# A ring of ten half places for the expert weights of a decoder layer, with the pair's products in another order

## The reference, cut to what matters

```python
h = h + merged @ w_out                       # end of the mixer
xt = rmsnorm(h, g_ffn)
logits = xt @ w_router + b_router            # top 4 of 32, softmax over the four
...
for each block of one expert e:              # rows = its tokens
    g = minimum(xb @ w_gate[e] + b_gate[e], 7.0)
    u = clip(xb @ w_up[e] + b_up[e], -7.0, 7.0)
    act = g * sigmoid(1.702 * g) * (u + 1.0)
    y[rows] += (act @ w_down[e] + b_down[e]) * wts
```

## Time and profile before

| | us |
|---|---|
| runs shown | 1229.80, 1230.49, 1230.92; median 1230.49 |
| profiled execution | 1230.71 |
| its span from the first to the last instruction | 1228.9 |
| PE busy | 1160.3 (94% of the span) |
| DMA, mean busy share of the 16 engines from about 305 to 1205 us | 0.98 to 1.03 |

### The profile page before, as it was taken

How to read it: one execution, slowest core, us unless ns; L and a number is a source line. 1 busy time by engine, 2 the same in 40 slices (tenths; PEclk the granted TensorE clock), 3 DMA queues, 4 the chain that set the end, 5 groups by cost and what they waited for, 6 DMA issues and landing times.

```text
span 1228.9 us, 13742 instructions
## 1 busy us (share of the span) xinstructions
PE 1160.3 (94%) x5460; PEld 586.8 (48%) x5460; DVE 446.5 (36%) x775; ACT 249.7 (20%) x409; POOL 47.6 (4%) x72
## 2 busy tenths in 40 slices
PE   8999999999999999999999899989999989899998
PEld 5888888787343443434343333424343424343433
DVE  4878798765312131231312131212222121212122
ACT  5555577632110100010010001000110000010000
POOL 2222100200000000000000000000000000000000
PEclk9999999999999999999999999999999999999999
DMA  9454545487999999999999999999999999999994
GB/s 374 146 197 171 189 154 206 169 341 305 429 422 428 428 431 429 437 428 429 438 430 428 434 434 428 430 437 430 428 433 434 429 429 434 434 425 436 434 423 189
DMA packets 28143, 458.59 MB, mean 373 GB/s; under 512 B 3216, under 2 KB 4112, under 8 KB 6608
## 3 DMA queue, kind: packets, MB, share of 16 engines
q1 hardware_dynamic: 26720, 454.14, 87.7%
q0 software_dynamic: 1104, 3.93, 1.0%
q10 hardware_dynamic: 288, 0.10, 0.0%
HBM read 457.11 MB, written 1.05 MB: 373 GB/s over the span
## 4 chain that ended last, share of the span: by engine, by line
PE 66%; DMA 27%; DVE 4%; ACT 1%; issue 1%; POOL 0%; SPq 0%; DVEq 0%; POOLq 0%
PE bank L1712 26%; DMA experts_ring<-in_w_up 25%; PE bank L1423 16%; PE bank L1754 11%; PE bank L1700 4%; PE bank L1640 3%; DMA back<-in_mixer_halves 2%; PE bank L1718 2%; PE bank L1387 1%; DVE back_split L913 1%; PE bank L1719 1%; DVE region L1337 1%; ACT region L891 0%; ACT region L896 0%; ACT back_split L653 0%
## 5 line engine op out<-in xcount | busy, mean ns | idle before, releaser
L1712 PE MATMUL bank<-experts_ring,region 128*64 128x512 f32 x2048 | 455.1, 597 | 28.2 <-DMA experts_ring<-in_w_up 14.4
L1712 PEld LDWEIGHTS bank<-experts_ring,region 128*64 128x64 f32 x2048 | 148.3, 137 | 312.1 <-issue 290.2
L1754 PE MATMUL bank<-experts_ring,region 128*64 128x512 f32 x1024 | 226.8, 595 | 14.3 <-ACT region L891 14.3
L1423 PE MATMUL bank<-back_split,region_split 128*128 128x512 f32 x600 | 176.6, 396 | 0.2
L1754 PEld LDWEIGHTS bank<-experts_ring,region 128*64 128x64 f32 x1024 | 75.6, 137 | 143.1 <-issue 129.1
L1423 PEld LDWEIGHTS bank<-back_split,region_split 128*128 128x128 f32 x600 | 110.5, 188 | 25.1 <-issue 2.0
L1372 DVE COPY region<-bank 64x512 f32<-64x512 f32 x32 | 22.2, 694 | 227.3 <-PE bank L1754 227.3
L913 DVE TENSOR_TENSOR back_split<-back,back_split 128x2048 fp32r<-128x2048 f32 x34 | 77.9, 2291 | 32.4 <-ACT back_split L653 32.2
L1423 PE MATMUL bank<-back_split,front_split 128*128 128x512 f32 x216 | 84.4, 391 | 0.0
L1361 DVE TENSOR_SCALAR region<-bank 128x512 f32<-128x512 f32 x32 | 22.1, 691 | 163.4 <-PE bank L1719 163.4
L884 ACT ACTIVATE region<-region 128x512 f32<-128x512 f32 x32 | 20.1, 630 | 292.0 <-DVE region L1354 292.0
(11 more groups left out here) (174 smaller groups left out, 790.1 us busy)
## 6 DMA issues: line engine op xcount, KB each, us to landing
experts_ring<-in_w_gate SPq DMA_DIRECT2D x26, 4096.0 KB, 32.5
experts_ring<-in_w_up SPq DMA_DIRECT2D x22, 4096.0 KB, 33.9
experts_ring<-in_w_down SPq DMA_DIRECT2D x20, 4096.0 KB, 35.1
experts_ring<-in_w_down SPq DMA_DIRECT2D x24, 2048.0 KB, 21.4
experts_ring<-in_w_up SPq DMA_DIRECT2D x20, 2048.0 KB, 16.0
back<-in_mixer_halves SPq DMA_DIRECT2D x36, 1024.0 KB, 4.8
experts_ring<-in_w_gate SPq DMA_DIRECT2D x12, 2048.0 KB, 12.3
front<-in_mixer_halves SPq DMA_DIRECT2D x8, 1024.0 KB, 4.8
```

Source lines behind the costliest of these rows:

```text
L1423: ins = nc.tensor.matmul(UB[u % 3][:, :], a[:, k, toks], b[:, cols], start=(k == 0 and m == 0), stop=(k == k_n - 1 and m == 2))
L1712: ins = nc.tensor.matmul(dst[h * SLOTS:(h + 1) * SLOTS, :], XE[:, kk, e * SLOTS:(e + 1) * SLOTS], w[:, k, h * HALF:(h + 1) * HALF], start= ...
L1754: ins = nc.tensor.matmul(bank[2][h * SLOTS:(h + 1) * SLOTS, :], AHT[:, k, half * SLOTS:(half + 1) * SLOTS], w[:, k, h * HALF:(h + 1) * HAL ...
```

## The change

The ring has ten half places instead of nine, so no piece wraps, and a load waits for half `g-10`. The mixer's buffers lie in SBUF in another order, and the small expert tiles have moved into regions that the ring does not cover. The first two pairs (`BY_HALVES`) and the whole last pair go by halves, the very last half as two quarters; pieces between are whole. The first halves are released otherwise: g=1 behind the load of H=39, g=2 behind that of H=40, g=3 after `wba1`, g=4 to 8 one after the other as halves of `wo0` and `wo1` are used, g=9 after the logits. The biases are loaded right behind g=0.

On PE, the dispatch of the next pair follows the first gate product; the wait for the upper half of the tokens stands between the halves of that product; combining is cut in two, one part behind the first up product and one inside the second gate product; the first turned activations come before the second up product, the second ones inside the first down product, through bank 0 and a second copy `AHT[1]`; the second down product has bank 1. The final combining uses four banks. GpSimd's clearing of `PWT` waits for the routing.

```diff
-RING = 9
+RING = 10
-TURN_PAIRS = 3
+TURN_PAIRS = 5
+BY_HALVES = 2 * PER_PAIR
+LAST_PAIR = PER_ROUND - PER_PAIR
...
+        buffers = ("region9", "mem_low", "x_low", "region7", "hi4", "raw4", "region8", "hi0", "raw0", "hi1",
+                   "raw1", "hi2", "raw2", "hi3", "raw3", "region1", "region10", "region2",
+                   "region0", "region5", "region3", "region4", "region6")
...
             def stream(pair, n, was_used):
-                if place(2 * n) == RING - 1:
-                    for g in (2 * n, 2 * n + 1):
-                        sp.wait_ge(used, was_used + (g + 1 - RING))
-                        load_half(pair, g)
-                else:
-                    sp.wait_ge(used, was_used + (2 * n + 2 - RING))
-                    load_piece(pair, n)
+                sp.wait_ge(used, was_used + (2 * n + 2 - RING))
+                load_piece(pair, n)
...
-                for n in range(TURNS * PER_TURN // 2, PER_ROUND // 2 - 1):
-                    stream(PAIRS - 1, n, was_used)
-                for g in (PER_ROUND - 2, PER_ROUND - 1):
+                for g in range(LAST_PAIR, PER_ROUND - 1):
                     sp.wait_ge(used, was_used + (g + 1 - RING))
                     load_half(PAIRS - 1, g)
+                sp.wait_ge(used, was_used + (PER_ROUND - RING))
+                rest = expert_rows(PAIRS - 1, PER_ROUND // 2 - 1)[:, 4096:8192]
+                for i in range(2):
+                    part = slice(i * 2048, (i + 1) * 2048)
+                    sp.dma_start(ring_half(PER_ROUND - 1)[:, part], rest[:, part]).then_inc(last_in[PER_PAIR - 1 + i], 16)
             for H in range(HALVES, 2 * N0):
                 load(H)
                 if H == 2 * PIECES.index("wba1"):
                     sp.wait_ge(pv_done, HEADS)
                     sp.wait_ge(merged, 4)
                     load_half(0, 0)
+                    biases()
+                if H == 2 * PIECES.index("wba1") + 1:
+                    sp.wait_ge(oT_done, HEADS)
+                    load_half(0, 1)
                 if H == 2 * PIECES.index("wo0"):
                     sp.wait_ge(unit_done, UNIT_OF[("ga1", NT - 1, 0)] + 1)
-                    biases()
-                    load_half(0, 1)
-            for g, name in enumerate(("wba1", "merged", "wo0", "wo0", "wo1", "wo1", "logits"), 2):
...
+                    load_half(0, 2)
+            sp.wait_ge(unit_done, UNIT_OF[("wba1", NT - 1, 0)] + 1)
+            load_half(0, 3)
+            sp.wait_ge(mgT_done, 4)
+            half_free(sp, 2 * PIECES.index("wo0"))
+            load_half(0, 4)
+            half_free(sp, 2 * PIECES.index("wo0") + 1)
+            load_half(0, 5)
+            half_free(sp, 2 * PIECES.index("wo1"))
+            load_half(0, 6)
+            half_free(sp, 2 * PIECES.index("wo1") + 1)
+            load_half(0, 7)
+            load_half(0, 8)
+            sp.wait_ge(logit_done, NT)
+            load_half(0, 9)
...
             def pair_products(r, d, s):
                 it = r * PAIRS + d * TURN_PAIRS + s
                 pe.wait_ge(xe_lo, it + 1)
-                pe.wait_ge(xe_hi, it + 1)
-                project(it, r, d, s, 0, 0, 0, bank[0])
+                project(it, r, d, s, 0, 0, 0, bank[0], lambda: pe.wait_ge(xe_hi, it + 1))
+                dispatch(it + 1)
...
+                pe.wait_ge(o_lo, it * 2 + 2)
+                pe.wait_ge(o_hi, it * 2 + 2)
                 project(it, r, d, s, 0, 1, 2, bank[1])
-                combine(it)
+                combine(it, 0)
                 pe.wait_ge(g_read, it * 2 + 1)
-                project(it, r, d, s, 1, 0, 4, bank[0])
+                project(it, r, d, s, 1, 0, 4, bank[0], lambda: combine(it, 1))
                 pe.wait_ge(u_read, it * 2 + 1)
+                pe.wait_ge(act_ready, it * 2 + 1)
+                pe.wait_ge(wT_copied, it + 2)
+                turn4(bank[3], [AH[:, j * P:(j + 1) * P] for j in range(4)], actT_done)
                 project(it, r, d, s, 1, 1, 6, bank[1])
                 for e in range(2):
-                    pe.wait_ge(act_ready, it * 2 + (e + 1))
-                    if e == 0:
-                        pe.wait_ge(wT_copied, it + 2)
-                    turn4(bank[3], [AH[:, e, j * P:(j + 1) * P] for j in range(4)], actT_done)
-                    if e == 0:
-                        dispatch(it + 1)
-                    if e == 1:
-                        pe.wait_ge(o_lo, it * 2 + 3)
-                        pe.wait_ge(o_hi, it * 2 + 3)
                     pe.wait_ge(actT_copied, it * 2 + (e + 1))
...
+                        if j == 8:
+                            pe.wait_ge(act_ready, it * 2 + 2)
+                            turn4(bank[0], [AH[:, b * P:(b + 1) * P] for b in range(4)], actT_done)
...
-            combine(n_rounds * PAIRS)
+            for j in range(4):
+                t, h = divmod(j, 2)
+                if j < 2:
+                    pe.wait_ge(y_added, last * 4 + (j + 1))
+                nc.tensor.matmul(bank[(6, 7, 0, 2)[j]][:, :], PWT[:, t * P:(t + 1) * P], OE[:, h * HALF:(h + 1) * HALF],
+                                 start=True, stop=True).then_inc(comb_done, 1)
```

More of the change, by code:

```diff
@@ L191, in decoder_layer @@
             named("attention_buffers", [P, 4096])
[L192 to L195, removed]
+            plain = {name: named(name, [P, 2048]) for name in buffers}
+            extra = named("extra", [P, HALF])
+            con = named("con", [P, C_ALL])
         prob = sb("prob", [P, 2, 768])
@@ L199, in decoder_layer @@
         rot = sb("rot", [P, 2, 2, NT, HD])
[L200 to L211, removed]
+        split_of = {name: sb(name + "_split", [P, 2048], F32R) for name in buffers}
+        extra_r = sb("extra_split", [P, HALF], F32R)
+        sb("con_kept", [P, C_MASK])
+        con_r = sb("con_split", [P, HALF], F32R)
+        region = [plain[f"region{i}"] for i in range(11)]
+        region_r = [split_of[f"region{i}"] for i in range(11)]
         small = sb("small", [P, 68])
@@ L330, in decoder_layer @@
         second_in = [sem(f"second_in{i}") for i in range(RING)]
-        last_in = [sem(f"last_in{i}") for i in range(2)]
+        last_in = [sem(f"last_in{i}") for i in range(PER_PAIR + 1)]
         gbias_in = [sem(f"gbias_in{i}") for i in range(3)]
@@ L396, in place @@
             return g % RING
-        whole_starts = [place(2 * n) for n in range(PER_ROUND // 2 - 1)]
+        whole_starts = [place(2 * n) for n in range(LAST_PAIR // 2)]
         def in_round(s):
@@ L413, in wait_half @@
             n, h = divmod(g, 2)
-            if n == PER_ROUND // 2 - 1:
-                pe.wait_ge(last_in[h], r * 16 + 16)
+            if g >= LAST_PAIR:
+                pe.wait_ge(last_in[g - LAST_PAIR], r * 16 + 16)
             elif h == 0:
                 pe.wait_ge(piece_in[place(g)], landed(r, d, n))
-            elif place(g) == 0:
-                pe.wait_ge(second_in[RING - 1], landed(r, d, n))
-            elif n < PER_TURN // 2:
+            elif g < BY_HALVES:
                 pe.wait_ge(second_in[place(g - 1)], 16 * whole_starts[:n + 1].count(place(g - 1)))
@@ L458, in load_half @@
                 n, h = divmod(g, 2)
-                if n == PER_ROUND // 2 - 1:
-                    landing = last_in[h]
+                if g >= LAST_PAIR:
+                    landing = last_in[g - LAST_PAIR]
                 else:
@@ L524, in _ @@
                         load_piece(0, n)
-                    load_half(0, RING - 1)
-                    sp.wait_ge(used, r * PER_ROUND + 1)
-                    load_half(0, RING)
-                    for n in range(RING // 2 + 1, PER_TURN // 2):
+                    for n in range(RING // 2, PER_TURN // 2):
                         stream(n // (PER_PAIR // 2), n, r * PER_ROUND)
@@ L859, in logit_exp, with xe_lower_half @@
                 nc.scalar.activation(GATE[:, t, :], LG[:, t, :], ACT.Exp, bias=stat[:, 180 + t:181 + t]).then_inc(lexp_done, 1)
-            def xe_lower_half(n):
+            def xe_lower_half(n, after):
                 act.wait_ge(disp_done, n * 2 + 1)
+                if after is not None:
+                    act.wait_ge(used, after)
                 nc.scalar.activation(XE[:, 0:4, :], bank[4][:, :].rearrange("p (k n) -> p k n", k=4),
@@ L890, in _ @@
                             act.wait_ge(actT_done, it * 2 + (e + 1))
-                            nc.scalar.activation(AHT, bank[3][:, :].rearrange("p (j s) -> p j s", j=4),
+                            nc.scalar.activation(AHT[e], bank[(3, 0)[e]][:, :].rearrange("p (j s) -> p j s", j=4),
                                                  ACT.Copy).then_inc(actT_copied, 1)
                             if e == 0:
-                                xe_lower_half(it + 1)
+                                xe_lower_half(it + 1, it * PER_PAIR + 8)
+                        for e in range(2):
                             act.wait_ge(used, it * PER_PAIR + (10 + 2 * e))
```

(14 more changed lines are left out.)

99 lines of the change are left out of this document (48 added, 51 removed).

## The result

The changed kernel takes 1233.15 us (median of 14 runs, 1231.63 to 1235.05), the kernel before 1230.22 (14 runs, 1228.48 to 1232.49). The ratio is 1.0022, 95% interval [1.0015, 1.0029]: slower by 0.22%, about 2.7 us by the ratio (the medians differ by 2.9). The forecast was 1226.2 in a range of 1220 to 1229.5, so the time lies above the range. The profiled execution took 1235.05 us with a span of 1233.3.

What follows compares the result with a forecast made beforehand. Weight DMA was taken to bound the experts, PE the end. Last landing 1212.5 + 4.9 - 4.9 + 2 = 1214.5; plus 2.4 + 7.7 gives span 1224.6, plus 1.8 - 0.2 gives 1226.2 us; range 1220 to 1229.5.

Steps and rivals of the forecast that it cites:

- the layout ... nothing: Whole kernel: the buffers' new layout, with GpSimd's later clearing, moved biases and split token wait, changes the time by nothing.
- Earlier expert halves: Mixer's end: g=2 ahead of H=41 delays S, the first expert product, by 4.9 us, 311.55 to 316.4; bounds 0 and 4.9.
- The step on H=40: Mixer's end: H=40 lands about 6 us later, but its split is done before H=41 arrives.
- The queue's order: SP's load queue at the mixer's end: loads land in order of issue, and no landing overtakes another.
- rival (a): Mixer's end: H=41 is not held up, S stays at 311.55, E is 4.9 us earlier, time 1221.3; chance 0.17.
- The dispatch moves forward: First pairs: 3.57 us of dispatch delay giving back ring places, so E, the last weight landing, is 2 us later; bounds 0, 3.3.
- The prediction's own test: Sign that the middle was wrong: DMA share under 0.95 anywhere from 330 to 450 us.
- The tenth place: Start of the expert stream: nine other halves issued instead of eight, so E comes 4.9 us earlier; bounds 0 and 4.9.
- Whole pieces from the third pair: Third pair on: a whole piece waits for two places at once; cost taken as 0, bounds 0 and 3.5 us.
- Less waiting within a pair: Expert pairs: 16 x 0.9 us of waits for ACT's copy and gaps in combining go, worth nothing until the last pair.
- rival (c): Expert pairs: PE becomes the bound, a pair taking over 58.4 us instead of the 54 expected; 1242 us; chance 0.08.
- The last pair and the banks: Kernel's end: last product at E + 2.4, final combining in four banks 7.7 us to the end, instead of 8.1.

Runs made afterwards that it cites:

- e3: The kernel before with only PE's loop over turns written out, so its instructions stream in: 1235.5 us, ratio 1.0048 to the kernel before.
- e5: Changed kernel with g=1, g=2 and biases released as before the change and the dispatch back behind the second up product: 1224.48 us, 0.9953 of the kernel before.
- e7: Changed kernel with nine half places, three-pair turns, the old release of early loads and dispatch behind the second up product: 1225.52 us, 0.9963 of the kernel before.
- e8: Changed kernel with only the bias loads put back behind H=40, g=1 and g=2 still early: 1232.61 us, 1.0016 of the kernel before.
- e9: Changed kernel with only the dispatch moved back behind the second up product, early releases kept: 1230.9 us, 1.0002 of the kernel before.
- e2: Changed kernel with g=1, g=2 and the biases released as before the change: 1228.78 us, 0.9984 of the kernel before.
- e1: Changed kernel with only g=2 moved back behind wba1, just ahead of g=3: 1231.36 us, 1.0003 of the kernel before.
- e6: Changed kernel with nine half places, three-pair turns and the old release of early loads, dispatch still early: 1227.73 us, 0.9977 of the kernel before.
- e4: The kernel before with only its last pair by halves and the last half in two quarters: 1227.0 us, 0.9971 of the kernel before.

## Why the prediction was wrong, by its steps

**The five-pair loop** is the step that cost the forecast most. It was not a term at all: the diff's `TURN_PAIRS = 5` was read as bookkeeping of the ring, and "the layout ... nothing" was where it belonged. From the 36th landing to the last the kernel before takes 758.3 us, the changed kernel 764.3: 6.0 us, where the forecast had none. e3 shows 5.2 of it without any other change, e5 against e7 5.4.

**Earlier expert halves** (S + 4.9): direction right, size wrong in the profile, where S came 8.2 later. The step that failed is the price, "One more half of 2 MB ahead of it costs 4.9 us": H=41 took 6.8 us longer (14.90 instead of 8.09) and was issued 0.4 later. At most about 1 us of the difference is the biases' place (e8); the rest stays open. Behind that, one tile of the dispatch took 3.16 us instead of 2.03, at the lower granted clock again (0.57 from 311 to 315 us): 1.1 of the 8.2. Why the clock fell there, with PE busy for 5.0 of the 6 us ahead of it, no run tells. Other executions come nearer to the forecast: counted from the issue of H=38, S is 7.9 us later after and 5.1 in e9, with the same front, and the medians put the front at 4.7 us (after to e2) and 6.0 (e9 to e5).

The step on H=40, "its split is done before H=41's arrives", held in the changed kernel: H=40's lower part was ready at 270.6, 3.1 us before H=41 landed.

```profile
268.26 2.29 DVE L914 TENSOR_TENSOR raw_split<-raw,hi_split 128x2048 fp32r<-128x2048 f32 x1 [5.36 <-ACT hi_split L651]
```

But that hid a second loss. H=40 landed at 266.23, 8.4 later than before, and in e1, where H=41 is back at 266.85, it alone holds S 4.3 late. So g=1's move was not free, as the term had it.

**The queue's order** was read rightly for the halves: each one, of the mixer and of the experts, landed in the order of issue, and rival (a) did not come about. "No landing here overtakes" is too wide all the same. In the kernel before, the 128 KB load of `b_gate`, issued at 250.56 behind H=40, landed at 257.08, ahead of H=40 at 257.85, and it overtook the load ahead of it in all twelve kernels. That agrees with the Trainium skill ("DMA: Bandwidth & Descriptors", "Queues, rings and completion order"), which says that completion is not FIFO per issuing engine. Its advice to issue a DMA early ("Rules for kernel authors") is not borne out here: two loads issued early cost 0.38% by what stood behind them.

**The dispatch moves forward** (+2, bounds 0 and 3.3): within its bounds. g=15 lands at 359.91, S + 40.1, where the prediction had S + 40.4. It went no further than this half. Between 331.9 and 370.4 four landings of after come late, beyond the 4.89 us of a half, by 4.45 us in all, and moving the dispatch back within the new order shortens E − S by 3.0 to 3.9 us (e7, e5, e9). But the term is against the kernel before, which loses some there too: e6 with the early dispatch stands 1.5 us above e4 (E − S 902.2 and 900.7; nine places and the last pair by halves in both, the rest of the new order in e6 alone). The medians make it about 3: e6 is 0.7 us slower than e4 though its end is 2.4 shorter; their intervals overlap. The prediction's own test, a DMA share under 0.95, would have missed the dry places: the share is 0.98, and only the GB/s fall.

**The tenth place** (−4.9): right, 4.5 to 5.3 us by the 36th landing. That it came to nothing in the time is the loop that it forces.

**Whole pieces from the third pair** (0): right; that pair's 12 halves land in 58.3 us in after, e9 and e5, at the pace of 4.87 us a half.

**Less waiting within a pair, and rival (c)**: right; the pair takes 53.2 us of PE, under the 54 taken, and PE waits on loads, not on ACT's copy.

**The last pair and the banks** (end − E 10.1): right, 10.3.

The sum, by stretches of the two profiles: S + 8.2 (forecast + 4.9); from S to the 36th landing − 3.8, the place and the dispatch together (forecast − 4.9 + 2 = − 2.9); from there to the last landing + 6.0 (forecast 0). So E = 1212.5 + 8.2 − 3.8 + 6.0 = 1222.9 against the forecast 1214.5. Of the 8.4 between them 6.0 are the loop and 3.3 the front, less 0.9 by which the place and the dispatch did better. The profiled run also lay 1.9 above its median, so the forecast missed the median by 7.0, the span by 8.7.

## What to carry to other kernels

Before a load is issued earlier, list each load behind it in its queue and follow each to the engine that waits, not only the last one. When a buffer ring gets another size, look at how long the loop body becomes and at the row of instruction packets, and compare landings: the GB/s of a long window did not show the loss here. While a stream's queue is still shallow, work that frees no buffer belongs late in the round, and the GB/s column shows a dry queue where the busy share hides it.

## What was not expected of the hardware

Fetching instructions cost a stream that is bound by bytes several times its own bytes: e3's 24 packets of 16 KB more, 0.9 us at 431 GB/s, cost it 5.2 us behind the 36th landing. A loop body of three pairs needed no packet between 500 and 1190 us, or one near 1190 (e6, e7); one of five pairs 27 or 28. And a pause of PE of 4.64 us stood ahead of a stretch of 7 us at a granted clock of 0.52, so that products after a late load ran at half pace too; the chain did not go over them here.
